# A ninth row buffer and a fifth gather ahead in a two-layer encoder with a product-key expert layer

## The reference, cut to what matters

```
x = x + merged.astype(x.dtype) @ w_out[l]
x = x + peer_ffn(rms_norm(x, norm2_w[l]), w_query[l], sub_keys[l], expert_u[l], expert_v[l])
...
q = (xt @ w_query).reshape(T, PEER_HEADS, 2, PEER_HALF)
...                                   # top-16 of the pair sums give idx, their softmax gives g
hid = jax.nn.gelu(jnp.einsum('td,thkd->thk', xb, expert_u[ib]).astype(jnp.float32), approximate=False)
return jnp.einsum('thk,thkd->td', (gb * hid).astype(xb.dtype), expert_v[ib])
```

## Time and profile before

| what | value |
|---|---|
| time, median of 3 runs | 4051.21 us |
| lowest and highest | 4047.34, 4053.17 us |
| span of the profiled execution | 5878.7 us |
| its own time beside the span | none is recorded apart |
| mean granted PE clock in it | 0.555 of full speed |
| PE busy | 5726.4 us (97%) |
| DVE busy | 2887.4 us (49%) |
| ACT busy | 1648.5 us (28%) |
| POOL busy | 1285.3 us (22%) |
| HBM traffic | 1439.31 MB read, 246 GB/s over the span |

### The profile page before, as it was taken

The page is one execution under the profiler, slowest core; times in us unless marked ns, Lnnn a source line. Parts: engine busy times, 40 slices in busy tenths (PEclk is TensorE's granted clock), DMA queues, the critical chain, the costliest instruction groups (busy, mean ns, idle before and its releaser), DMA issues.

```text
span 5878.7 us, 40315 instructions
## 1 busy us (share of the span) xinstructions
PE 5726.4 (97%) x13374; PEld 2787.7 (47%) x13374; DVE 2887.4 (49%) x5745; ACT 1648.5 (28%) x4216; POOL 1285.3 (22%) x1094
## 2 busy tenths in 40 slices
PE   9999999999999998999999999899999999899999
PEld 5555555444444545444445545344445555222222
DVE  3321003665555455756555555756555554744443
ACT  3431101344422211244432211245422211222222
POOL 0000000222222221322222221322222221334343
PEclk6555555555555555555555555555555555555555
DMA  4222222767777775767777775777777775899997
GB/s 155 93 102 81 73 90 95 267 238 266 261 275 268 274 280 202 285 245 280 273 272 297 283 291 190 280 256 271 271 268 308 281 290 191 315 350 342 345 342 281
DMA packets 212948, 1444.45 MB, mean 246 GB/s; under 512 B 27256, under 2 KB 27256, under 8 KB 46340
## 3 DMA queue, kind: packets, MB, share of 16 engines
q0 software_dynamic: 164976, 1133.94, 52.0%
q1 hardware_dynamic: 47632, 307.80, 14.4%
q10 hardware_dynamic: 132, 0.12, 0.0%
HBM read 1439.31 MB, written 7.13 MB: 246 GB/s over the span
## 4 chain that ended last, share of the span: by engine, by line
PE 96%; DVE 2%; ACT 1%; issue 1%; DMA 0%; SPq 0%; ACTq 0%; DVEq 0%
PE banks L609 52%; PE sums L871 21%; PE banks L871 7%; PE banks L748 5%; PE banks L827 3%; PE banks L669 2%; PE banks L736 1%; PE banks L786 1%; PE banks L778 1%; PE banks L694 1%; PE banks L844 1%; DVE x L1479 1%; DVE rows L1470 0%; PE banks L637 0%; PE banks L700 0%
## 5 line engine op out<-in xcount | busy, mean ns | idle before, releaser
L609 PE MATMUL banks<-hT,ring 128*128 128x256 f32 x6656 | 2608.4, 583 | 4.7 <-DVE arena L1316 3.9
L609 PEld LDWEIGHTS banks<-hT,ring 128*128 128x128 f32 x6656 | 1507.5, 228 | 1151.7 <-issue 734.0
L576 POOL DMA_INDIRECT rows<-in_w_uv,idx x1024 | 1237.6, 1209 | 3600.3 <-PE sums L871 1981.3
L1470 DVE CUSTOM_DVE_ANT_0 rows<-rows,xn 128x1024 f32<-128x1024 f32 x1024 | 1241.6, 1220 | 530.8 <-DMA rows<-in_w_uv,idx 528.0
L871 PE MATMUL sums<-rows,diag 128*128 128x512 f32 x1612 | 1285.2, 970 | 70.0 <-ACT diag L1076 47.9
L1479 DVE SCALAR_TENSOR_TENSOR x<-rows,wgt,x 128x1024 f32<-128x1024 f32 x493 | 632.0, 1282 | 234.8 <-ACT wgt L1068 234.0
L871 PEld LDWEIGHTS sums<-rows,diag 128*128 128x128 f32 x1612 | 369.2, 232 | 791.7 <-issue 683.2
L1281 DVE SCALAR_TENSOR_TENSOR arena<-banks,pr,arena 128x254 f32<-128x254 f32 (+1 forms) x512 | 246.8, 482 | 354.6 <-ACT arena L965 340.9
L1063 ACT ACTIVATE gelu<-hid 128x2 f32<-128x2 f32 x512 | 102.9, 201 | 1100.7 <-DVE hid L1470 1099.3
L609 PE MATMUL banks<-yT,ring 128*128 128x256 f32 x1024 | 400.2, 582 | 0.0
L871 PE MATMUL banks<-rows,diag 128*128 128x512 f32 x512 | 393.7, 966 | 0.0
(11 more groups left out here) (205 smaller groups left out, 2955.8 us busy)
## 6 DMA issues: line engine op xcount, KB each, us to landing
ring<-in_w_ssd SPq DMA_DIRECT2D x96, 1024.0 KB, 5.4
ring<-in_w_att SPq DMA_DIRECT2D x64, 1024.0 KB, 6.1
ring<-in_w_mrg SPq DMA_DIRECT2D x52, 1024.0 KB, 8.4
arena<-a_rows POOLq DMA_DIRECT2D x32, 1024.0 KB, 7.6
ring<-in_w_qry SPq DMA_DIRECT2D x32, 1024.0 KB, 4.8
arena<-bias_tiles POOLq DMA_DIRECT2D x16, 1152.0 KB, 7.3
ring<-in_w_out SPq DMA_DIRECT2D x16, 1024.0 KB, 7.0
rows<-in_w_uv,idx POOLq DMA_INDIRECT x1024, 6.8
```

Source lines behind the costliest of these rows:

```text
L576: nc.gpsimd.indirect_dma_start(out=rows[n % NB][:, :], out_offset=None, in_=w_uv, in_offset=bass.IndirectOffsetOnAxis(ap=idx[:, t, s:s + 1 ...
L609: mm = pe.matmul(out, w[:, k * P:(k + 1) * P], rhs[:, k0 + k, :], start=start and k == 0, stop=stop and k == n - 1)
L1470: v.tensor_tensor_reduce(u, u, xn2[:, (n // SLOTS_T) % 3, :], 1.0, 0.0, ALU.mult, ALU.add, hid[:, k:k + 1]).then_inc(u_done, 1)
```

## The change: nine buffers, and where the room comes from

`NB` goes from 8 to 9, so `AHEAD` goes from 4 to 5. The room for 8 KB more per partition comes from smaller arrays: `xn2` has two buffers, `idx` and `gate` two tiles, `hid`, `gelu` and `wgt` are rings of `HID` = 16. The norm weights are no longer held in `n2b`: POOL loads them straight into the `xn2` buffer in which the normalised rows are then made in place. This takes one load for each tile in place of one for each pass. Tile 0's load is issued at position `out` 0.2 without waiting for x; tile 1's at `ssd` 0.3 of step 0 in the next pass. Tile 0's rows are made in `norm2` as before. Tile 1's reciprocal root is kept aside by a small copy (`keep_ok`), and its rows are made in `ssd` step 1 of the next pass (`late_rows`), for the last pass after slot 4 of the tail. `gates` waits on `g_w`, since a gate buffer is now used again after two tiles.

```diff
-NB = 8
+NB = 9
 LAG = 3
 AHEAD = NB - LAG - 1
...
+HID = 16
...
-        xn2 = sb("xn2", [P, 3, D])
-        idx = sb("idx", [P, NT, SLOTS_T], U32)
-        gate = sb("gate", [P, NT, SLOTS_T])
-        hid = sb("hid", [P, SLOTS_P])
-        gelu = sb("gelu", [P, SLOTS_P])
-        wgt = sb("wgt", [P, SLOTS_P])
+        xn2 = sb("xn2", [P, 2, D])
+        idx = sb("idx", [P, 2, SLOTS_T], U32)
+        gate = sb("gate", [P, 2, SLOTS_T])
+        hid = sb("hid", [P, HID])
+        gelu = sb("gelu", [P, HID])
+        wgt = sb("wgt", [P, HID])
...
+                if m:
+                    yield place("ssd", 0, 0.3)
+                    late_norm_rows(m - 1)
                 yield place("ssd", 0, 0.5)
                 pool.wait_ge(dt_T.sem, dt_T.at(m, 2))
...
-                yield place("norm2", 0, 0.2)
-                pool.wait_ge(x_mid.sem, x_mid.at(m, 2))
-                pool.dma_start(n2b, w_n2[m // 2].partition_broadcast(P)).then_inc(n2_in.sem, 16)
+                yield place("out", 0, 0.2)
+                if m:
+                    pool.wait_ge(u_done, SLOTS_P * (m - 1) + SLOTS_T)
+                norm_rows(m, 0)
+
+            def norm_rows(m, t):
+
+                pool.dma_start(xn2[:, t, :], w_n2[m // 2].partition_broadcast(P)).then_inc(n2_in.sem, 16)
+
+            def late_norm_rows(m):
+
+                if m:
+                    pool.wait_ge(u_done, SLOTS_P * m)
+                norm_rows(m, 1)
...
+            late_norm_rows(PASSES - 1)
+            pool.wait_ge(xn_ok.sem, xn_ok.at(PASSES - 1, 1))
...
+                if m:
+                    v.wait_ge(g_w, SLOTS_P * (m - 1) + SLOTS_T * (t + 1))
...
+            def rows_of(m, t, scale):
+
+                v.wait_ge(n2_in.sem, n2_in.at(m, 16 * (t + 1)))
+                v.scalar_tensor_tensor(out=xn2[:, t, :], in0=x[:, 2 * (m % 2) + t, :], scalar=scale, in1=xn2[:, t, :],
+                                       op0=ALU.mult, op1=ALU.mult).then_inc(xn_ok.sem, 1)
+
+            def late_rows(m):
+
+                v.wait_ge(keep_ok, m + 1)
+                rows_of(m, 1, stat[:, 32:33])
...
+                        if m and g == 1:
+                            late_rows(m - 1)
...
-                v.wait_ge(n2_in.sem, n2_in.at(m, 16))
-                for t in range(2):
-                    if m:
-                        v.wait_ge(u_done, SLOTS_P * (m - 1) + SLOTS_T)
-                    v.scalar_tensor_tensor(out=xn2[:, (2 * m + t) % 3, :], in0=x[:, 2 * b + t, :], scalar=stat[:, 12 + t:13 + t], in1=n2b,
-                                           op0=ALU.mult, op1=ALU.mult).then_inc(xn_ok.sem, 1)
+                rows_of(m, 0, stat[:, 12:13])
+                v.tensor_copy(stat[:, 32:33], stat[:, 13:14]).then_inc(keep_ok, 1)
...
+                if k == 4:
+                    late_rows(PASSES - 1)
```

More of the change, by code:

```diff
@@ L327, in build @@
         junk = cut(D)
-        n2b = cut(D)
-        after_n = used[0]
         first = rows[NB - 1]
@@ L445, in build @@
         sg_ok, m_v, mT_ok = count("sg_ok", 16), count("m_v", 24), count("mT_ok", 8)
-        out_mm, x_mid, n2_in = count("out_mm", 1), count("x_mid", 2), count("n2_in", 16)
+        out_mm, x_mid, n2_in = count("out_mm", 1), count("x_mid", 2), count("n2_in", 32)
         q_ev, q_s, q_sv = count("q_ev", 16), count("q_s", PH), count("q_sv", PH)
-        k_v, i_ok, s_d, s_e, s_v2 = (sem(n) for n in ("k_v", "i_ok", "s_d", "s_e", "s_v2"))
+        k_v, i_ok, s_d, s_e, s_v2, keep_ok = (sem(n) for n in ("k_v", "i_ok", "s_d", "s_e", "s_v2", "keep_ok"))
         xn_ok = count("xn_ok", 2)
@@ L562, in mixer @@
                     bias_tiles(hp)
-                yield place("norm2", 0, 0.2)
-                pool.wait_ge(x_mid.sem, x_mid.at(m, 2))
-                pool.dma_start(n2b, w_n2[m // 2].partition_broadcast(P)).then_inc(n2_in.sem, 16)
+                yield place("out", 0, 0.2)
[8 more added lines that the diff above has]
+                norm_rows(m, 1)
             def gather(n):
                 p, k = n // SLOTS_P, n % SLOTS_P
-                t = 2 * (p % 2) + k // SLOTS_T
-                s = k % SLOTS_T
+                t, s = k // SLOTS_T, k % SLOTS_T
                 if k == 0 or part_of(p, k) != part_of(p, k - 1):
@@ L589, in _ @@
             together(mixer, tick)
-            pool.wait_ge(xn_ok.sem, xn_ok.at(PASSES, 0))
+            late_norm_rows(PASSES - 1)
+            pool.wait_ge(xn_ok.sem, xn_ok.at(PASSES - 1, 1))
             pool.dma_start(wfin, w_final.partition_broadcast(P)).then_inc(f_w, 16)
@@ L1060, in tick @@
                 n = p * SLOTS_P + k
-                t = 2 * (p % 2) + k // SLOTS_T
+                t = k // SLOTS_T
+                c = (n - 1) % HID
                 act.wait_ge(u_done, n + 1)
-                act.activation(gelu[:, k - 1:k + 1], hid[:, k - 1:k + 1], ACT.Gelu).then_inc(g_ge, 1)
+                act.activation(gelu[:, c:c + 2], hid[:, c:c + 2], ACT.Gelu).then_inc(g_ge, 1)
                 act.wait_ge(g_ge, n // 2 + 1)
@@ L1067, in tick @@
                 for q in (k - 1, k):
-                    act.activation(wgt[:, q:q + 1], gelu[:, q:q + 1], ACT.Copy,
+                    h = q % HID
+                    act.activation(wgt[:, h:h + 1], gelu[:, h:h + 1], ACT.Copy,
                                    scale=gate[:, t, q % SLOTS_T:q % SLOTS_T + 1]).then_inc(g_w, 1)
@@ L1075, in tick @@
                             act.wait_ge(v_pe, e - DIAGS + 1)
-                        act.activation(diag[e % DIAGS][:, :], ident, ACT.Copy, scale=wgt[:, q:q + 1]).then_inc(d_ok, 1)
+                        act.activation(diag[e % DIAGS][:, :], ident, ACT.Copy, scale=wgt[:, q % HID:q % HID + 1]).then_inc(d_ok, 1)
             def final(s, t):
@@ L1199, in route @@
                     link(v.tensor_scalar(row[t][:, ks], idh[t][:, 0, ks], float(P), float(l * EXPERTS), ALU.mult, ALU.add))
-                    v.tensor_tensor(idx[:, 2 * b + t, ks], row[t][:, ks], idh[t][:, 1, ks], ALU.add).then_inc(i_ok, 1)
+                    v.tensor_tensor(idx[:, t, ks], row[t][:, ks], idh[t][:, 1, ks], ALU.add).then_inc(i_ok, 1)
                     if n:
@@ L1213, in gates @@
                 v.wait_ge(s_v2, 3 * n + 2)
-                v.tensor_tensor(gate[:, 2 * (m % 2) + t, ks].rearrange("p (h k) -> p h k", h=hi - lo), Ge[:, hs],
+                if m:
+                    v.wait_ge(g_w, SLOTS_P * (m - 1) + SLOTS_T * (t + 1))
+                v.tensor_tensor(gate[:, t, ks].rearrange("p (h k) -> p h k", h=hi - lo), Ge[:, hs],
                                 spread(grec[:, hs], 2, TOPK), ALU.mult).then_inc(s_v2, 1)
+            def rows_of(m, t, scale):
[5 more added lines that the diff above has]
+                rows_of(m, 1, stat[:, 32:33])
             def mixer(m):
@@ L1469, in tick @@
                 u = rows[n % NB][:, 0:D]
-                v.tensor_tensor_reduce(u, u, xn2[:, (n // SLOTS_T) % 3, :], 1.0, 0.0, ALU.mult, ALU.add, hid[:, k:k + 1]).then_inc(u_done, 1)
+                v.tensor_tensor_reduce(u, u, xn2[:, k // SLOTS_T, :], 1.0, 0.0, ALU.mult, ALU.add, hid[:, k % HID:k % HID + 1]).then_inc(u_done, 1)
                 for q in sums_after(k):
@@ L1478, in tick @@
                         v.wait_ge(v_dve, dve_sums(p, q) - 1)
-                    v.scalar_tensor_tensor(out=xo, in0=rows[before % NB][:, D:], scalar=wgt[:, q:q + 1], in1=xo,
+                    v.scalar_tensor_tensor(out=xo, in0=rows[before % NB][:, D:], scalar=wgt[:, q % HID:q % HID + 1], in1=xo,
                                            op0=ALU.mult, op1=ALU.add).then_inc(v_dve, 1)
```

## The result

The changed kernel takes 4065.4 us (median of 6 runs, 4060.25 to 4067.49), the kernel before 4051.31 us (6 runs): ratio 1.0037, 95% interval 1.0027 to 1.0047. Forecast was 4034 us, faster.

A forecast was written before the change was run, and what follows sets the result against it. DMA was taken to bound the mixers and the tail of the timed run. Ninth buffer -23, norm weight loads +5, copy +1 gave -17 us: 4051 to 4034 us, own range 4010 to 4043, overall 3990 to 4070.

The forecast's parts named there:

- The rebuilding of the timed run: Whole kernel: clock-independent parts of the slow profile split 4051 us into 580 + 60, three mixers of 895, tail 725.
- the share of 0.91: Tail: DMA engines busy 0.91 of 797 us in the slow profile, so at least 725 us if they bound it.
- A ninth buffer and AHEAD 5: Mixers: one more slot carried over each stall, 2.6 us each, nine stalls: 23 us gained; tail nothing.
- `out`, `query` and the change of pass: The three stalls per mixer where the ninth buffer was to let in one more gather, 2.6 us each.
- The loads of norm weights: Second load per pass: four more DMAs of 512 KB, between 0 and 5 us, taken as 5 us lost.
- DVE's moved operation and copy: Tile 1's operation moves from `norm2` to `ssd` step 1, taken as 0; the copy costs 1 us at most.
- the added waits: Waits on g_w, keep_ok and u_done are for things finished long before: cost 0.
- Saturated: Mixers: DMA can keep up only 393 GB/s, no idle time to win, 4056 us; chance 0.25 together with PE-bound.
- Behind one more gather: `ssd` step 0: decay-row DMAs queue behind one more gather, 16 us lost, 4072 us; chance 0.15.
- Its own sign: DVE's mask waits for decay rows growing well beyond 37 us would show the queue rival at work.
- Loop-bound: Mixers: slots paced by buffer turn, not bandwidth; ninth buffer wins 72 us, 3984 us; chance 0.10.
- PE as the bound at 0.8: Timed runs bound by PE at a clock of some 0.8: 4051 + 1; within the no-gain chance of 0.25.

The follow-up runs named there:

- the second profile: The kernel before, unedited, profiled again at a higher clock: 4052.2 us, span 4050.3 us, clock 0.944.
- f2_before_shifted: The kernel before with 192 unused bytes per partition ahead of diag and the row buffers: 4075.58 us, ratio 1.0062.
- f1_after_padded: The changed kernel with 320 unused bytes per partition, so that its row buffers start at a multiple of 512 again: 4039.51 us, ratio 0.9975.
- f3_eight_buffers_padded: The changed kernel with eight buffers and 320 unused bytes per partition that realign the row buffers: 4057.78 us, ratio 1.0021.
- e1_eight_buffers: The changed kernel with NB = 8, so AHEAD = 4, all else of the change kept: 4083.92 us, ratio 1.0082.
- e2_nine_buffers_four_ahead: The changed kernel with nine buffers but AHEAD = 4: 4063.74 us, ratio 1.0034.
- e3_before_with_second_load: The kernel before with a second 512 KB load of norm weights per pass, in `norm2`: 4050.12 us, ratio 1.0004.
- m1_tile0_load_back: f1_after_padded with tile 0's norm weight load put back in `norm2` behind the wait for x_mid: 4031.62 us, ratio 0.9948.
- g2_late_rows_big_rings: The changed kernel with eight buffers and HID = 256, which aligns the row buffers by itself: 4056.52 us, ratio 1.0017.
- g1_small_rings_only: The kernel before with only the change's small arrays and the wait on g_w, row buffers kept aligned: 4048.21 us, ratio 0.9996.
- m4_tile1_later: f1_after_padded with tile 1's load moved behind the broadcast of step 2 and its rows to step 4: 4038.47 us, ratio 0.9971.

## Why the prediction was wrong, step by step

The rebuilding of the timed run from a trace at another clock held in the order of the limits, less so in their sizes. I had pass 0 at 580 + 60 = 640 us, the second profile has 639.2. I had 895 us per mixer, it has 935, 912 and 917; I had the tail at 725 us, it has 648. Both errors have one cause: I took the share of 0.91 in the earlier trace rows as a limit on the tail, while gathers alone run at 427 GB/s there when PE is fast enough, not at the 404 that I went by. That rate stood in the earlier trace rows too; I passed it over for the lower one. PE has 773 to 794 us of work in a mixer, not at most 719, since its clock there is 0.93.

In the mixers the DMA engines are busy nearly always (share 0.95 to 0.96), as said. That is not yet a limit: they move 385 to 393 GB/s there, and the chain of the second profile has DMA on 30% of the span, DVE on 27% and PE on 24%. How much the gathers' rate counts can be read from f2_before_shifted, which is the kernel before with slower gathers and the same program: in the profiled executions its mixers take 7.5, 7.0 and 3.2 us longer, its tail 9.5, for 256 slots each. So the gathers' rate counts in the mixers for some six tenths of what it does in the tail, an estimate from one execution of each.

The step that failed is the sum's silence on addresses: the part "A ninth buffer and AHEAD 5" counts a slot as the same 2.6 us of DMA time before and after. The gathers became 1.3% slower because three arrays in front of their buffers shrank to 64 bytes each. That term is +26 us (f1_after_padded against the change, and f2_before_shifted against before), more than my largest term, and none of the rivals had it. The diff showed it: three sizes change from a multiple of 1024 bytes to 64, and what is allocated behind them moves.

The ninth buffer: -23 us forecast, -19 measured with the shift and -18 without. The size was near, and partly by luck. Right was that the gain lies in the mixers and not in the tail: from eight padded buffers (f3_eight_buffers_padded) to nine the mixers go from 938.2, 914.3 and 912.3 us to 934.7, 906.9 and 907.4, the tail from 649.4 to 649.9. Right was also that the buffer carries a slot over a stall; DVE waits for gathers 22 us less in all, and at most 2.9 us in place of 4.7 (us, times, longest; first eight padded buffers, then nine):

```profile
DVE rows L1496 <- DMA rows<-in_w_uv,idx: 520.6, 421, 4.7
```

```profile
DVE rows L1496 <- DMA rows<-in_w_uv,idx: 498.2, 399, 2.9
```

Wrong was where. I had named `out`, `query` and the change of pass. The dot products laid side by side, for this pair and for e1_eight_buffers against the changed kernel, show the gain of mixers 2 and 3 in two places: 2 to 4 us between slots 56 and 64, in `ssd`, and 2 to 3 us between slots 104 and 128, where `att` begins (mixer 1 has 4 us at the second place and nothing at the first). From slot 208 to 240, that is in `out`, `norm2` and `query`, it lies between 0.9 us won and 2.1 lost. The last 8 slots before the change of pass give 1.1 to 1.3 us each time, not 2.6. The first place in mixer 2, slot 63, on DVE (start, us, what, idle before), with eight padded buffers and with nine:

```profile
1801.15 1.23 DVE L1496 CUSTOM_DVE_ANT_0 rows<-rows,xn 128x1024 f32<-128x1024 f32 x1 [3.72 <-DMA rows<-in_w_uv,idx]
```

```profile
1795.66 1.22 DVE L1496 CUSTOM_DVE_ANT_0 rows<-rows,xn 128x1024 f32<-128x1024 f32 x1
```

With eight it waits 3.72 us for the gather, with nine not at all. That AHEAD was not needed for the gain (e2_nine_buffers_four_ahead) I had not foreseen. The mixers and the tail of the padded change:

```profile
1570.70:2477.60 906.90, 771.69 (x3168) 555.77 (x3168) 763.21 (x1470) 410.47 (x1022) 317.79 (x271) 0.93 0.97 395
2477.60:3385.00 907.40, 774.57 (x3168) 558.26 (x3168) 763.17 (x1470) 409.97 (x1021) 322.82 (x273) 0.93 0.96 392
3385.00:4034.90 649.90, 487.74 (x1024) 191.06 (x1024) 346.42 (x626) 179.14 (x662) 252.00 (x251) 0.96 0.98 415
```

The loads of norm weights: +5 us taken, for bytes. The bytes cost nothing that can be measured where the kernel before has them (e3_before_with_second_load). What costs is the place of tile 0's load: in `out`, 7 to 8 us by m1_tile0_load_back. All late rows and loads together cost 5 to 8 us by g2_late_rows_big_rings and f3_eight_buffers_padded, so nothing else of size is left in them. I had argued that issuing it early covers its landing, and so it does, nobody waits for it; that this is not all a load can cost is what I had missed. Why the place costs that much is open: three or four loads of 0.5 MB at 427 GB/s would be 4 to 5 us if nothing hid them, but the faster kernel moves the same bytes. I did not test more.

DVE's moved operation and copy, the added waits and the small rings: 0 to 1 us taken; g1_small_rings_only and m4_tile1_later show nothing that can be measured.

The rivals. Saturated: half right, DMA is nearly always busy in the mixers, and still a buffer won 19 us. Behind one more gather, priced at 16 us: refuted by e2_nine_buffers_four_ahead, which takes that gather away and is 2 us faster than the change. Its own sign did not come either: DVE's mask waits 34.5 us for the decay rows in the changed kernel, 42.3 in the kernel before at the same clock. Loop-bound, with its 72 us: refuted, the ninth buffer took 16 us from the mixers of the profiled executions. PE as the bound at 0.8: refuted by the clock of 0.944 and PE at 84%.

The account from the runs: -19 (ninth buffer, unpadded as in the change) + 26 (start of the buffers) + 7 to 8 (tile 0's load) = +14 to +15 us; measured +14.

## What to carry to other kernels

When a diff changes the size of any on-chip array, compute where the arrays allocated behind it now start, and above all where large DMAs land. A 320-byte unused tensor was worth more here than the buffer that the whole change was made for. And test the parts of a change that "makes room" without its purpose: eight buffers in the new layout showed in one run that 34 us were lost and 19 won.

A profile at another clock can be turned into the timed run's limits by bytes and by durations that don't depend on the clock, but the rate of one of its stretches is only a lower bound for the timed run. The 404 GB/s that I picked was too low; the best 20 us of the same trace had the 427 that the second profile shows inside the tail.

## What the runs showed of the hardware that was not expected

Indirect gathers of 8 KB rows run at 427 GB/s into buffers that start at 0 or 256 bytes past a multiple of 512, and at 421 to 422 GB/s at 64, 128 or 192 past: 0.6% of this kernel's time. Plain 1 MB loads 128 bytes past a multiple of 512 showed no such loss within 2 us. Packets of 8 KB on SP's queue took 309 ns with and without that shift. And 427 GB/s held through 400 us of a single core's gathers, well above the 358 that the Trainium skill names in "DMA: Bandwidth & Descriptors", Bandwidth, for a core beside a loaded neighbour.
